# Angles of the rotation tables on GpSimd, and the norm of mem inside the first input product with half of its columns in another pair of buffers

## The reference, cut to what matters

```python
def rms_norm(x, g, eps=NORM_EPS):
    xf = x.astype(jnp.float32)
    y = xf * lax.rsqrt(jnp.mean(xf * xf, axis=-1, keepdims=True) + eps)
    return (y * g.astype(jnp.float32)).astype(x.dtype)

def rope_tables(positions, dim):
    inv_freq = ROPE_THETA ** (-jnp.arange(0, dim, 2, dtype=jnp.float32) / dim)
    ang = positions.astype(jnp.float32)[..., None] * inv_freq
    return jnp.cos(ang), jnp.sin(ang)

def cross_attention(h, m, w_q, w_kv, w_o):
    ...
    kv = (m @ w_kv).reshape(Bn, m.shape[1], 2, CROSS_HEADS, CROSS_HEAD_DIM)
    ...

def first_block(...):
        cos, sin = rope_tables(positions, HEAD_DIM)
        h = rms_norm(x, g_mix[l])
        proj = h @ w_in[l]
        ...
        x = x + cross_attention(rms_norm(x, g_cross[l]), rms_norm(mem, g_mem[l]),
                                w_cq[l], w_ckv[l], w_co[l])
```

## Time and profile before

| | before |
|---|---|
| time, median of 3 runs | 1575.82 us (1574.57 to 1583.59) |
| the profiled execution's own time, its span | 1585.44 us, 1583.7 us |
| PE busy | 1470.7 us, 93% |
| DVE, ACT, POOL busy | 68%, 46%, 4% |

### The profile page before, as it was taken

The page is one execution under the profiler, slowest core; times in us unless marked ns, Lnnn a source line. Parts: engine busy times, 40 slices in busy tenths (PEclk is TensorE's granted clock), DMA queues, the critical chain, the costliest instruction groups (busy, mean ns, idle before and its releaser), DMA issues.

```text
span 1583.7 us, 18472 instructions
## 1 busy us (share of the span) xinstructions
PE 1470.7 (93%) x7116; PEld 1216.0 (77%) x7116; DVE 1070.5 (68%) x1438; ACT 727.0 (46%) x1064; POOL 67.7 (4%) x109
## 2 busy tenths in 40 slices
PE   4988789899999999989889999899998989899998
PEld 3776667788887888878778888688887868688886
DVE  3687675667677766776657666777767778676445
ACT  5444454544436434454454333444334756353443
POOL 4000000000001000010000000000000000000000
PEclk9999899999999999999699999999999999899999
DMA  7753052577766777846148779678776630475651
GB/s 250 257 204 112 28 181 84 187 265 266 277 228 194 264 263 261 265 165 180 55 158 290 251 257 255 207 241 283 256 238 214 179 110 1 133 241 171 208 187 70
DMA packets 189116, 314.25 MB, mean 198 GB/s; under 512 B 6960, under 2 KB 100455, under 8 KB 189031
## 3 DMA queue, kind: packets, MB, share of 16 engines
q1 hardware_dynamic: 148528, 231.82, 45.5%
q10 hardware_dynamic: 38678, 76.69, 13.4%
q0 software_dynamic: 1824, 4.57, 0.9%
HBM read 311.99 MB, written 1.07 MB: 198 GB/s over the span
## 4 chain that ended last, share of the span: by engine, by line
PE 79%; DVE 9%; ACT 4%; issue 3%; POOL 2%; DMA 2%; ACTq 0%; DVEq 0%; POOLq 0%
PE ps L998 23%; PE ps L1000 23%; PE ps L999 22%; PE ps L1007 5%; PE ps L1297 2%; DVE wlo L958 2%; PE ps L1134 1%; PE ps L1252 1%; ACT whi L949 1%; DVE xn L1704 1%; DMA qT<-in_ada_w 1%; DVE tmp L1738 1%; DVE rmax L2029 1%; DMA raw<-in_nsa_w_out 1%; DVE sp L2026 1%
## 5 line engine op out<-in xcount | busy, mean ns | idle before, releaser
L958 DVE TENSOR_TENSOR wlo<-raw,whi 128x2048 fp32r<-128x2048 f32 (+1 forms) x221 | 501.6, 2271 | 179.9 <-ACT whi L949 179.2
L998 PE MATMUL ps<-whi,aT 128*128 128x512 f32 (+1 forms) x1216 | 493.5, 406 | 36.3 <-DVE aTl L1726 28.1
L1000 PE MATMUL ps<-wlo,aT 128*128 128x512 f32 (+1 forms) x1216 | 480.4, 395 | 0.0
L999 PE MATMUL ps<-whi,aTl 128*128 128x512 f32 (+1 forms) x1216 | 479.6, 394 | 0.0
L949 ACT ACTIVATE whi<-raw 128x2048 fp32r<-128x2048 f32 (+1 forms) x221 | 418.7, 1895 | 118.9 <-PE ps L1000 81.1
L998 PEld LDWEIGHTS ps<-whi,aT 128*128 128x128 f32 x1216 | 234.6, 193 | 85.0 <-issue 41.2
L1000 PEld LDWEIGHTS ps<-wlo,aT 128*128 128x128 f32 x1216 | 234.2, 193 | 49.7
L999 PEld LDWEIGHTS ps<-whi,aTl 128*128 128x128 f32 x1216 | 235.3, 193 | 43.7
L998 PE MATMUL ps<-whi,hT 128*128 128x512 f32 (+1 forms) x524 | 200.2, 385 | 2.2 <-ACT z L1537 1.4
L1000 PE MATMUL ps<-wlo,hT 128*128 128x512 f32 (+1 forms) x524 | 197.4, 379 | 0.0
L999 PE MATMUL ps<-whi,hTl 128*128 128x512 f32 (+1 forms) x524 | 197.0, 378 | 0.0
(11 more groups left out here) (230 smaller groups left out, 1296.4 us busy)
## 6 DMA issues: line engine op xcount, KB each, us to landing
raw<-in_ff_w SPq DMA_DIRECT2D x176, 512.0 KB, 4.8
raw<-in_ff_w SPq DMA_DIRECT2D x44, 1024.0 KB, 5.2
qT<-in_ada_w ACTq DMA_DIRECT2D x36, 1024.0 KB, 6.1
pT<-in_ada_w ACTq DMA_DIRECT2D x36, 1024.0 KB, 7.3
raw<-in_w_up SPq DMA_DIRECT2D x16, 1024.0 KB, 5.7
raw<-in_w_down SPq DMA_DIRECT2D x16, 1024.0 KB, 5.0
raw<-in_w_in SPq DMA_DIRECT2D x9, 1024.0 KB, 7.2
raw<-in_w_ckv SPq DMA_DIRECT2D x8, 1024.0 KB, 5.4
```

The lines of the kernel that those rows point to most:

```text
L958: dve.tensor_tensor(wlo[:, slot, 0:m], raw[:, slot, 0:m], whi[:, slot, 0:m].bitcast(F32), ALU.subtract).then_inc(w_lo, 1)
L998: pe.matmul(out_ap, hi, w, start=start, stop=False)
L999: pe.matmul(out_ap, lo, w, start=False, stop=False)
L1000: return pe.matmul(out_ap, hi, wl, start=False, stop=stop)
```

## The change

Two edits. The 19 instructions for the angles leave DVE and become 21 on POOL, behind the norm of x (`scalar_tensor_tensor` becomes a multiplication and an addition, with a new scratch `kc_`). And the norm of mem is taken apart: `norm_scale` becomes `norm_rows` (scaling) and `norm_turn` (transposes, for a part of the columns). Sums of squares stand now at unit 3 of "w_in", the scaling at unit 4, the first half (chunks 0 to 3, into `hT`, `hTl`) at unit 5; only the second half (chunks 4 to 7, into `aT`, `aTl`) stays between the linears. "w_ckv" takes its left side from both pairs (`lhs="ha"`). In the second block `latent_norms` is written with the new functions; order and number of its instructions per engine are those of before.

```diff
@@ Plan
+        left = {"a": self.left, "h": self.left_h, "ha": self.left_h + self.left[4:8]}[lhs][chunk0:chunk0 + kcs]
...
-    def norm_scale(self, st):
+    def norm_rows(self, st):
         for who in "AD":
             self.n_xn[who] += 1
...
+    def norm_turn(self, st, col0=0, width=None, **to):
+
+        st = dict(st, col0=col0, width=width or st["width"], lo0=self.norm_rounds, hi0=self.n_hi, **to)
+        st["rounds"] = self.rounds((st["width"] // P + 1) // 2, "D")
...
@@ make_plan
-    p.linear(A["w_in"][0], D, 2304, "z", "w_in", tables=True)
+    mem = []
+
+    def mem_stats():
+        mem.append(p.norm_stats("mem", D, ("prm", G_MEM), eps=1e-5))
+
+    def mem_rows():
+        p.norm_rows(mem[0])
+
+    def mem_first():
+        p.norm_split(p.norm_turn(mem[0], 0, 512, to="h", chunk0=0))
+
+    p.linear(A["w_in"][0], D, 2304, "z", "w_in", tables=True, inner={3: mem_stats, 4: mem_rows, 5: mem_first})
     after_in = p.last_fill
-    p.norm("mem", D, ("prm", G_MEM), eps=1e-5)
-    p.linear(A["w_ckv"][0], D, 2 * D, "zc", "w_ckv", side=after_in, flush=7)
+    p.norm_split(p.norm_turn(mem[0], 4, 512, to="a", chunk0=4))
+    p.linear(A["w_ckv"][0], D, 2 * D, "zc", "w_ckv", side=after_in, flush=7, lhs="ha")
...
@@ DVE, tables(): the 19 instructions from tensor_copy(posf) to the clipping of ang are taken out
@@ POOL
+            def turns_less(c):
+                g_step(pool.tensor_scalar(flat(kc_), flat(kk), -c, None, ALU.mult))
+                g_step(pool.tensor_tensor(flat(ang), flat(kc_), flat(ang), ALU.add))
+
+            def tables():
+
+                pool.wait_ge(small_loaded, 16 * N_SMALL)
+                g_step(pool.tensor_copy(posf[:, :, :], pos[:, :, :]))
+                for k in range(2):
+                    for tt in range(NT):
+                        for i, (f0, f1) in enumerate(((0, 32), (32, 48))):
+                            n = g_count(pool.tensor_scalar(ang[:, k, tt, f0:f1], freq[:, f0:f1], posf[:, i, tt:tt + 1], None, ALU.mult))
+                pool.wait_ge(g_done, n)
+                for k in range(2):
+                    n = g_count(pool.tensor_scalar(flat(kk[:, k]), flat(ang[:, k]), 1 / TWO_PI, 0.25 if k == 0 else 0.0, ALU.mult, ALU.add))
+                pool.wait_ge(g_done, n)
+                g_step(pool.tensor_scalar(flat(kk), flat(kk), MAGIC, None, ALU.add))
+                g_step(pool.tensor_scalar(flat(kk), flat(kk), -MAGIC, None, ALU.add))
+                for c in (C1, C2):
+                    turns_less(c)
+                g_step(pool.tensor_scalar(flat(ang[:, 0]), flat(ang[:, 0]), math.pi / 2, None, ALU.add))
+                turns_less(C3)
+                pool.tensor_scalar(flat(ang), flat(ang), -PI_LOW, PI_LOW, ALU.max, ALU.min).then_inc(ang_ready, 1)
+
...
                 elif st["kind"] == "edge":
                     edge(st)
+                    if st["acc"] is None:
+                        tables()
```

More of the change, by code:

```diff
@@ L529, in latent_norms @@
             def latent_norms():
+                turned = []
                 for st in latents:
-                    p.norm_scale(st)
-                for st in latents:
+                    p.norm_rows(st)
+                    turned.append(p.norm_turn(st))
+                for st in turned:
                     p.norm_split(st)
@@ L1105, in linear @@
                                 kc = c0 + k0 + k
+                                hi, lo = lhs[kc]
                                 if b == 0:
@@ L1367, in cmp_out @@
                     last.then_inc(t_ready, 1)
-            table = dict(params=params, edge=edge, edge_post=edge_post, norm_scale=norm_scale, linear=linear, mlp=mlp, qk1=turns_of, qk_cross=turns_of,
+            table = dict(params=params, edge=edge, edge_post=edge_post, norm_turn=norm_turn, linear=linear, mlp=mlp, qk1=turns_of, qk_cross=turns_of,
                          q_mla=turns_of, k_mla=turns_of, q_nsa=turns_of, k_nsa=turns_of, w_nsa=turns_of,
@@ L1662, in cmp_hid @@
                     act.activation(hid_rows[0:32, kv, :], tbank(t)[0:32, 0:P], ACT.Silu).then_inc(t_act, 1)
-            table = dict(edge=edge, edge_post=edge_post, norm_stats=norm_stats, norm_scale=norm_scale, norm_split=norm_split,
+            table = dict(edge=edge, edge_post=edge_post, norm_stats=norm_stats, norm_rows=norm_rows, norm_split=norm_split,
                          linear=linear, mlp=mlp, qk1=turns_of, qk_cross=turns_of,
@@ L1791, in tables @@
                 dve.wait_ge(small_loaded, 16 * N_SMALL)
[L1793 to L1803, removed]
-                for c in (C1, C2):
-                    link(dve.scalar_tensor_tensor(flat(ang), flat(kk), -c, flat(ang), ALU.mult, ALU.add))
-                link(dve.tensor_scalar(flat(ang[:, 0]), flat(ang[:, 0]), math.pi / 2, None, ALU.add))
-                link(dve.scalar_tensor_tensor(flat(ang), flat(kk), -C3, flat(ang), ALU.mult, ALU.add))
-                dve.tensor_scalar(flat(ang), flat(ang), -PI_LOW, PI_LOW, ALU.max, ALU.min).then_inc(ang_ready, 1)
                 for i in range(2):
```

42 lines of the change are left out of this document (20 added, 22 removed).

## The result

| | before | after |
|---|---|---|
| time, median, first comparison (20 runs each) | 1581.76 us (1574.57 to 1592.19) | 1571.69 us (1563.4 to 1579.94) |
| the profiled execution's own time, its span | 1585.44, 1583.7 us | 1570.92, 1569.2 us |
| PE busy | 1470.7 us | 1459.5 us |

The changed kernel takes 0.994 of the time before, 95% interval 0.9922 to 0.9958: 9.5 us less, 6.6 to 12.3. The forecast was 11.85 us less. It lies in both intervals, but the time itself was forecast as 1564.0 us and came out as 1571.69, near the upper end of the range. Of the 7.7 us between the two, 5.9 are the level that the forecast started from (1575.82 against 1581.76), and 1.8 are what the change gave less than forecast, which the interval cannot tell from nothing.

What follows compares the result with a forecast made beforehand. PE, busy 93% of the span, was taken as the bound, with two early stalls. 5.15 + 7.2 - 0.5 = 11.85 us off the median 1575.82 gave 1564.0 us, range 1559.5 to 1572.0.

Steps and rivals of the forecast that it cites:

- the level: Starting time for the whole kernel: median 1575.82 us, with the profiled execution, 1585.4, taken as 9.6 above it.
- First stall and its clock: PE's 3.70 us wait before unit 6 of "w_in" and 2.65 of slow clock behind it shrink: 5.15 us gained.
- The hole: PE's gap between "w_in" and "w_ckv", 8.33 us with its clock, shrinks to 1.1: 7.2 us gained.
- POOL, 0.5 us: POOL's angle instructions beside DVE at the norm of x: 0.5 us lost, nearest to the row where only POOL waited.
- The 3 us that I worked out from the rule as an upper case: By the port lock, five DVE instructions at 22.6 to 34 us lose up to 0.6 each; time would be 1566.4.
- the cover of 21 us: Angles ready on POOL by 35 us at the latest, while ACT needs them at 56.3.
- What lies behind moves as a whole: Everything behind "w_ckv" waits for its results, so it moves earlier as a whole.
- the first stall stays: Rival: ACT comes some 2 us later, PE stands 2.3 us, first term shrinks to 0.5; 1568.6 us; chance 0.12.
- POOL holds DVE: Rival: at the norm of x POOL delays DVE by 3 to 4 us; 1567 to 1568 us; chance 0.10.
- the gain is given back in "w_ckv": Rival: DVE can't keep up with an early PE there, the 7.2 us go; 1571.2 us; chance 0.05.
- Late angles: Rival: POOL's two-input instructions cost 40 us each, sine 93 us late, 1657 us; gain gone at 68; chance 0.03.
- More than forecast: Rival: later stalls end at another phase of the clock's steps, bringing a few us; below 1560; chance 0.05.

Runs made afterwards that it cites:

- e8: The kernel before again, unedited, profiled a second time on another chip than the first four follow-up runs; 1583.3 us, one run.
- e3: Changed kernel, but all eight chunks of mem transposed between the linears into one pair of buffers; 1581.12 us, ratio 0.9967 to before.
- e5: The changed kernel again, unedited, for a second profile and comparison; 1574.21 us against 1587.2 before, ratio 0.9911.
- e6: Changed kernel with POOL's tables waiting only until DVE has scaled both row tiles of x; 1575.35 us, ratio 0.9908 to before.
- e4: Changed kernel with POOL's tables held until DVE has made all four rests of x; 1576.17 us, ratio 0.9948 to before.
- e7: Changed kernel with POOL computing the angle tables three times over on the same buffers, so they come late; 1585.79 us, ratio 0.9998 to before.
- e1: Changed kernel with the norm of mem put back between the linears, only the angles on POOL; 1582.9 us, ratio 0.9987 to before.
- e2: Changed kernel with the angles back on DVE, only the norm of mem taken apart; 1584.24 us, ratio 0.9986 to before.

## Why the prediction was right or wrong

**The step that failed: the level.** The sum, 11.85 us, was taken off 1575.82, the median of three runs, because the profiled execution (1585.44) was taken for one that lay 9.6 us too high. It was the three that lay low, by chance: two of them are the lowest of the first comparison's 20 runs. The level came out as 1581.76, 5.94 us higher, and as 1587.15 over 35 runs and 1587.2 over 17 on other occasions; none of those 52 later runs is at or below 1575.82. 1581.76 - 11.85 would have been 1569.9, against 1571.69 measured. What is left, 1.8 us, is the sum itself: 11.85 forecast, 10.1 measured as a difference of medians and 9.5 by the ratio, both within what the measurement can't tell apart. Counting the profiled execution as a fourth run would have said as much beforehand: the median of the four is 1579.7.

**First stall and its clock, 5.15 us.** The mechanism held: the copy at 61.46 (61.2 forecast, without POOL's half), unit 6 at 62.17 (61.9), and the transposes cover the gap. PE stood for nothing there, where 0.3 was forecast, because it was itself 0.46 us later at the end of unit 5. At the end of "w_in" the gain is 84.24 - 79.35 = 4.89 us, POOL's loss included; the forecast with it was 4.65. Against e8, which was quicker behind the same stall, it is 83.23 - 79.35 = 3.88. The 2.65 for the clock was the price in one execution; in the other the clock was 0.68 over the 5.3 us, 1.7 us.

**The hole, 7.2 us.** From PE's last `ada_out` group to "w_ckv" it was 92.32 - 84.24 = 8.08 us and is 80.74 - 79.35 = 1.39: 6.69, and 0.75 for the clock, 7.4. The forecast start, 80.7, came out at 80.74. That it fits so well is in part luck: 80.7 left POOL's 0.5 us out, and the first stall and the hole, each 0.2 us better than forecast, made up for it. e3 shows that some 2.5 us of this need the second pair of buffers.

**POOL, 0.5 us.** Right in size (0.52, and 0.67 in e5), and for the reason that the nearest row spoke against. The row at 18.73 had shown only POOL waiting: it ended at 19.54, not with DVE's subtraction (19.36) but one instruction of 0.18 us behind it, and there DVE had started first. With the tables there DVE waits as well, 0.15 and 0.36 us on the two instructions ahead of PE's transposes. The Trainium skill (page "SBUF — State Buffer", section "SBUF: two separate sides") says that a DVE instruction in a two-port mode or with two inputs in SBUF and a GpSimd instruction exclude each other, and that the one that starts first keeps the shared pair of ports for its whole instruction. The trace agrees that both wait, and that POOL waits out DVE's instruction (2.74 against 0.69). It does not show DVE held for the whole of POOL's: the subtraction at 34.57 in e6 lost 0.18 us behind an instruction that had 0.68 to go, and at 28.42 DVE lost 0.15 where POOL's went on to 29.06. The 3 us that I worked out from the rule as an upper case didn't come: DVE loses at most 0.39 us at a time in these profiles (DVE's sum of squares of mem at 50.55 in e4, 1.62 against 1.23), often nothing, and in its long subtractions it is mostly POOL that waits. POOL's prices were too low in part: 0.39 us for each of the eight small ones (0.3 at most forecast), 0.70 for 192 columns with one input (0.44, in proportion from another operation), 0.59 with two (0.6). The end, 34.71, lies at the edge of the 29 to 35 that was given; the cover of 21 us made it harmless.

**What lies behind.** "What lies behind moves as a whole" held: PE has no idle time in "w_ckv", unit 8's rest was ready at about 71.7 (71.4 forecast), and the attention starts 12.3 us earlier than in the first profile, 10.5 us earlier than in e8.

**The rivals.** That the first stall stays, that POOL holds DVE for 3 to 4 us, and that the gain is given back in "w_ckv" are excluded by the waits and stretches above. Late angles were shown by e7: the loss begins near 56.9 (e4) and runs at about 1 us per us (12.1 us for 10.8, the clock included; these are two points). The gain over before is used up at 67.7, where 68 was forecast. "More than forecast" was based on phases of the clock. These do exist, as e8 and e1 show, but they hit the kernel before too. The price of "POOL holds DVE back" was off by a little as well: 3 to 4 us in place of 0.5 give 1566.5 to 1567.5, not 1567 to 1568.

One number's row is missing ahead of the prediction: the earlier trace rows was cited for `ada_q` at 0.75 us each, and that figure stands in the costliest groups of the page of before:

```profile
L1918 DVE SCALAR_TENSOR_TENSOR qT<-qT,cact 128x512 f32<-128x512 f32 x108 | 80.9, 749 | 2.6
```

**What stays open.** Whether 1 or 2 us of the head's 11 are lost later can't be told: the two comparisons give 9.5 and 14.1, with intervals of about 3 and 5 us to either side. Nor is it known how often the changed kernel suffers e1's loss at 30 us, or whether the late `hidc` of e4 to e7 has to do with the edits.

## What to carry to other kernels

Take the level from all runs that you have, the profiled one too; three runs of a kernel that spreads over 18 us don't make a level, and a forecast of a difference should be kept apart from it. When two stalls sit on one engine's queue, walk the queue of the engine that is late with both edits in it: here the norm moved forward alone made the first stall longer, and the angles moved alone left the hole. Work handed to GpSimd cost half a microsecond here where DVE was busy for 55% of the time, took 1.2 to 1.6 times as long where DVE was busy for 67 to 76%, and it holds DVE up in return, so put it behind the DVE instructions that something waits for, and well before its own deadline.

## What the runs showed of the hardware

- POOL and DVE make each other wait. The chain of tables took 13.9 us with DVE busy for 32% of the time (e7's third pass), 14.2 with 55% (the changed kernel, from 20.5), 17.7 with 67% (e6, from 29.6), 20.0 with 71% (e7's second pass) and 22.3 with 76% (e4, from 34.5). In e7's third pass, from 59.7 on, when DVE did nothing, each instruction of 192 columns but the last took 0.59 to 0.70 us.
- Eight transposes between products, and stops of 0.9 and 0.8 us (e3, at the linears) and of 1.25 to 1.76 (the changed kernel and e3, at 29 us), left the granted clock at 1.00. Behind stops of 2.20 (e1), 3.4 (e2), 3.70 (before) and 9.42 us (e7) it went to its lower level, 1.2 GHz, at once or within the next 1.3 us. One and the same stop had different prices: the 3.70 us cost 2.65 us of clock in one execution and 1.7 in another, and the hole 0.75 in the first profile of before and 2.0 in e1.
- A clock that rises early can bring on its own loss: in e1 it rose some 2 us sooner than in the changed kernel, PE ran out of work sooner, stood 2.20 us instead of 1.25, and was set back to 0.50 for 3.1 us. In e4, with the same early rise and POOL out of the way, it stood 1.58 us and kept its clock. These rises are read from the distance of the products (0.43 and 0.23 us); the granted clock is given as 1.00 in every profile up to its first fall, also where the products come at the slow pace.
- The spread between executions goes with the clock. Over the 35 runs of before, a mean granted clock lower by 0.01 goes with 15.6 us more, and a straight line through them accounts for 86% of the variance; over the 20 of the changed kernel it is 12.5 us and 80%. This is a correlation: no run sets the clock.
